# A two-layer hybrid block on one core: the tiles that TensorE reads laid at distances from the weights that are odd multiples of 32 bytes

## What is computed

```python
for l in range(2):
    x = x + 0.5 * swiglu_ffn(rms_norm(x, ffn1_norm[l]), ffn1_w_gu[l], ffn1_w_down[l])     # 1024 -> 2 x 2816 -> 1024
    h = rms_norm(x, mix_norm[l])
    (x_r, g_r, q_b, c_kv, q_i, k_i, w_i, q_c, k_c, v_c, f_c, gate_a, gate_b, gate_c) = split(h @ w_in[l])
    merged = (sigmoid(gate_a) * (rglru_branch(...) @ w_branch[l, 0])
              + sigmoid(gate_b) * (dsa_branch(...) @ w_branch[l, 1])
              + sigmoid(gate_c) * (fox_branch(...) @ w_branch[l, 2]))
    x = x + merged @ w_out[l]
    x = x + memory_cross_attention(rms_norm(x, xattn_norm[l]), rms_norm(mem, mem_norm[l]), w_mq[l], w_mkv[l], w_mo[l])
    x = x + 0.5 * swiglu_ffn(rms_norm(x, ffn2_norm[l]), ffn2_w_gu[l], ffn2_w_down[l])
return rms_norm(x, final_norm)
```

## Time and profile before

| | before |
|---|---|
| median of 3 runs | 1412.49 us (1412.26 to 1412.88) |
| profiled execution | 1413.24 us, span 1411.4 us |
| TensorE: matmuls, weight loads | 97%, 87% of the span |
| VectorE, ScalarE, GpSimd | 67%, 55%, 9% |
| mean granted clock of TensorE | 0.994 |
| memory read | 241 MB, 172 GB/s over the span |

### The profile page before, as it was taken

How to read it: one execution, slowest core, us unless ns; L and a number is a source line. 1 busy time by engine, 2 the same in 40 slices (tenths; PEclk the granted TensorE clock), 3 DMA queues, 4 the chain that set the end, 5 groups by cost and what they waited for, 6 DMA issues and landing times.

```text
span 1411.4 us, 23830 instructions
## 1 busy us (share of the span) xinstructions
PE 1372.3 (97%) x8846; PEld 1224.1 (87%) x8846; DVE 944.3 (67%) x1456; ACT 777.2 (55%) x1378; POOL 131.2 (9%) x219
## 2 busy tenths in 40 slices
PE   6999989999999999999999999999999999999998
PEld 5888879988999888888888888898989989888886
DVE  5666665868666567666676666658777666666665
ACT  5555555745654466454565555466546445655554
POOL 4010000022420100000010000000224001100000
PEclk9999999999999999999999999999999999999999
DMA  8677664544545545666666667446454554466662
GB/s 240 189 205 208 199 177 150 180 125 151 174 135 174 180 139 175 183 193 193 179 179 193 194 178 221 136 138 203 129 162 138 163 195 145 127 207 179 196 190 75
DMA packets 286384, 243.38 MB, mean 172 GB/s; under 512 B 14344, under 2 KB 263608, under 8 KB 286304
## 3 DMA queue, kind: packets, MB, share of 16 engines
q1 hardware_dynamic: 284176, 236.77, 55.5%
q10 hardware_dynamic: 1600, 4.25, 0.9%
q0 software_dynamic: 528, 1.26, 0.5%
HBM read 241.18 MB, written 1.27 MB: 172 GB/s over the span
## 4 chain that ended last, share of the span: by engine, by line
issue 64%; PE 26%; DVE 3%; ACT 2%; POOL 2%; POOLq 1%; DVEq 1%; DMA 1%; ACTq 0%
PE work L1548 16%; PE work L1623 2%; PE work L1570 2%; PE acc L1585 1%; PE work L1627 1%; PE acc L1775 1%; POOL diag L721 1%; ACT w_hi L507 1%; PE work L1763 1%; DVE w_lo L515 1%; POOLq L720 1%; DVE score L1350 1%; PE work L1754 1%; PE work L1698 0%; PE acc L1499 0%
## 5 line engine op out<-in xcount | busy, mean ns | idle before, releaser
L515 DVE TENSOR_TENSOR w_lo<-raw,w_hi 128x1024 fp32r<-128x1024 f32 x444 | 549.6, 1258 | 104.2 <-ACT w_hi L507 102.3
L507 ACT ACTIVATE w_hi<-raw 128x1024 fp32r<-128x1024 f32 (+1 forms) x442 | 450.5, 1053 | 25.6 <-PE acc L1585 25.6
L1623 PE MATMUL work<-act,w_hi 128*128 128x512 f32 x1408 | 439.2, 393 | 9.5 <-DVE w_lo L515 5.5
L1627 PEld LDWEIGHTS work<-act,w_lo 128*128 128x128 f32 x1408 | 265.0, 188 | 59.2
L1548 PE MATMUL work<-act,w_hi 128*128 128x256 f32 x1696 | 312.0, 282 | 4.2 <-DVE act L1131 2.1
L1627 PE MATMUL work<-act,w_lo 128*128 128x256 f32 x1408 | 278.8, 279 | 0.0
L1548 PEld LDWEIGHTS work<-act,w_hi 128*128 128x128 f32 x1696 | 262.2, 188 | 11.0 <-issue 6.2
L1548 PE MATMUL work<-act,w_lo 128*128 128x256 f32 x848 | 236.7, 279 | 0.0
L1623 PEld LDWEIGHTS work<-act,w_hi 128*128 128x128 f32 x1408 | 216.5, 188 | 13.4 <-issue 10.4
L821 ACT ACTIVATE gu_s<-work 128x256 f32<-128x256 f32 x176 | 58.1, 382 | 199.1 <-PE work L1627 199.1
L1548 PEld LDWEIGHTS work<-act,w_lo 128*128 128x128 f32 x848 | 159.1, 188 | 0.6 <-issue 0.5
(11 more groups left out here) (238 smaller groups left out, 1746.0 us busy)
## 6 DMA issues: line engine op xcount, KB each, us to landing
raw<-in_ffn_w_gu SPq DMA_DIRECT2D x174, 512.0 KB, 5.0
raw<-in_w_in SPq DMA_DIRECT2D x52, 1024.0 KB, 5.2
raw<-in_ffn_w_down SPq DMA_DIRECT2D x44, 1024.0 KB, 4.9
raw<-in_w_branch SPq DMA_DIRECT2D x12, 1024.0 KB, 5.0
raw<-in_w_mkv SPq DMA_DIRECT2D x8, 1024.0 KB, 5.2
raw<-in_w_out SPq DMA_DIRECT2D x8, 1024.0 KB, 4.9
raw<-in_w_mq SPq DMA_DIRECT2D x4, 1024.0 KB, 5.4
raw<-in_w_mo SPq DMA_DIRECT2D x4, 1024.0 KB, 4.8
```

What stands on the lines that cost most here:

```text
L507: eng.activation(halves(w_hi, slot, kind, part), halves(raw, slot, kind, part), ACT.Copy)\
L515: eng.tensor_tensor(halves(w_lo, slot, kind, part), halves(raw, slot, kind, part), halves(w_hi, slot, kind, part).bitcast(F32), ALU.subtra ...
L1623: pe.matmul(work[:, 2 * c + g, :], w_hi[:, slot, at_w:at_w + P], act[:, :, k, :], start=(k == 0), stop=False, skip_group_check=True)
L1627: mm = pe.matmul(work[:, 2 * c + g, 0:SEQ], w_lo[:, slot, at_w:at_w + P], act_hi[:, k, :], start=False, stop=(k == KT - 1), skip_group_che ...
```

## The change

The order of the `at` calls. No instruction, wait, size or overlay differs, apart from the addresses. The 320, 224, 64 and 128 bytes of small tiles now lie between the big ones and shift them by 32 bytes modulo 64, and the 8192 bytes of `mem_x` (with `fox_bias` and `mrg_lo` over it) move from before the branch tiles to behind `pt`, the place of the products.

```diff
         x = at("x", [P, TT, D])
-        mem_x = at("mem_x", [P, TT, D])
-        fox_bias = at("fox_bias", [P, HEADS, SEQ], over="mem_x")
-        mrg_lo = at("mrg_lo", [P, KT, SEQ], F32R, over="mem_x")
+        mx = at("mx", [P, 4, 2])
+        nm = at("nm", [P, 4, 2])
+        gain = at("gain", [P, 5, KT])
         xr = at("xr", [P, BT, SEQ + CONV_W])
...
+        gains = at("gains", [P, 5, DEPTH, KT])
         act = at("act", [P, 2, KT, SEQ], F32R)
         act_hi, act_lo = act[:, 0, :, :], act[:, 1, :, :]
+        sm = at("sm", [P, 4, 2])
+        ri = at("ri", [P, 4, 2])
         o_hi0, o_lo0, o_hi1, o_lo1 = (at(name, [P, BT, SEQ], F32R) for name in ("o_hi0", "o_lo0", "o_hi1", "o_lo1"))
...
         lg = at("lg", [P, 2, 2, SEQ])
+        ch = at("ch", [P, 8, BT])
         pt = at("pt", [P, 2, 2, 2, P])
+        mem_x = at("mem_x", [P, TT, D])
+        fox_bias = at("fox_bias", [P, HEADS, SEQ], over="mem_x")
+        mrg_lo = at("mrg_lo", [P, KT, SEQ], F32R, over="mem_x")
...
-        gains = at("gains", [P, 5, DEPTH, KT])
-        gain = at("gain", [P, 5, KT])
-        ch = at("ch", [P, 8, BT])
...
-        mx = at("mx", [P, 4, 2])
-        nm = at("nm", [P, 4, 2])
-        sm = at("sm", [P, 4, 2])
-        ri = at("ri", [P, 4, 2])
```

## The result

The changed kernel takes 1429.18 us (median; 1427.44 to 1430.02) against 1412.38 before: a ratio of 1.0122, 95% interval 1.011 to 1.0135. It is slower by 17 us, where 24 us less had been forecast; the range held the time. The profiled execution has a span of 1428.2 us, 16.8 more than before.

The account below looks back on a forecast made before the run. The prediction took the pace of successive TensorE matmuls as the bound, not memory or waits. Gate and up 7.2, down 2.3, last down and output projections 2.5 and L1548 12.0 us summed to 24.0: 1412.5 - 24.0 = 1388.5 us, range 1372 to 1434.

Parts of the forecast that it names:

- (c): Tiles of VectorE, ScalarE and GpSimd move by 32 modulo 64: at most 3 us either way, taken as 0.
- (d): mem_x, fox_bias and mrg_lo go behind the products, small tiles fill gaps; same overlays and waits: 0.
- (a): Four big matmul groups move to distance 160 modulo 256; lower-end paces of 113.3 and 226.6 ns save 24.0 us.
- (b): Branch tiles moving, memory parts and act as stationary operand get other distances; counted nothing, bounds 5.7 us gain, 1.2 us cost.
- odd multiples of 32 are the bad phase: Rival, same four groups: one stall more per step, 21.7 us slower, 1434 us; chance 0.22.
- The distance doesn't count: Rival: starting phase or tile sizes set the matmuls' pace, so time stays 1412.5 us within 3; chance 0.15.
- the third rival: Stalls vanish altogether: fast-form matmuls reach the plain fp32 pace, 216.7 and 108.3 ns, 82 us less, 1330 us; chance 0.08.
- My picture of two reads that stall each other: Reading the next matmul's weights meets the running moving-operand read; short stalls explain pace differences of 3 to 7 ns.

Follow-up runs that it names:

- the sweep: TensorE matmuls alone on zeros, 24 per distance from 0 to 992 bytes: 512 columns take 229 ns at 192, 233 to 234 at most others.
- the two halves of the change: Kernel before with act alone moved: 1424.56 us, ratio 1.009; changed kernel with act back at 192: 1416.0 us, ratio 1.0024 to the kernel before.
- the last sweep: TensorE alone, moving operand alternating between two starts, then 248 to 512 columns, then plain float32: 256 columns at 192 took 113.3 ns over 24 steps.
- two sweeps: TensorE alone over distances, in steps of 32, then in steps of 8: gate and up pattern at 224 took 693.5 and 706.8 ns.

## Why the prediction was wrong

**What bounds the kernel: right.** The pace of the matmuls is the time. The waits of TensorE stayed where they were, and all engines' tiles could move by 32 modulo 64 for nothing, (c) and (d) of the prediction.

**That the pace goes with the distance modulo 256: right for this kernel's steps**, and shown by the sweep, by the two halves of the change and by the kernel with everything 32 bytes up. One shape at one clock takes 226.5 or 233.5 ns by addresses alone, and kernel and sweep agree on the size for 512 columns. It isn't the whole: at 256 columns what ran before and the moving operand's step change the pace as much. The plain form takes 215.8 ns at every distance.

The Trainium skill's rule ("SBUF — State Buffer", who interferes with whom), by which TensorE waits on nobody, is about other engines, and there the sweep agrees: 5.60 and 5.50 us at 160 and 192 with VectorE and ScalarE busy, 5.61 and 5.50 with both idle. That addresses don't matter, as the prediction drew from it, doesn't follow; the difference is there with TensorE alone. The Trainium skill's 2.5 ns over the columns' time for one matmul behind another ("TensorE: Matmul & The Clock Gate", back-to-back issue gap) agree with the plain form if a record counts as twice its columns, 213.3 and 426.7 ns, and not with the fast form.

**The step that failed is (a), the choice of the end.** The cost at 160 had been bounded by 113.3 and 120.0 ns (226.6 and 233.2), and I took the lower end because 160 is next to 192 and because 0 and 64 seemed the bad places. That took a curve for smooth of which three points were known, and read one of them wrongly: 0 is bad for 256 columns (120.0), but for 512 it is the best multiple of 32 (226.5). The merged sums, which mix 0 and 64, had hidden it. The sweep has it: from 192 to 160, 512 columns go from 229 to 233.5 and 256 columns from 117.8 to 120. The measured paces are at the upper bound in each of these groups. What the 113.3 of the earlier trace rows shows is a rhythm that a sequence at 192 can fall into, over 24 steps in the last sweep; at 160 the same unit takes 120.0.

Term by term, in the profile after:
- gate and up: 88 x 0.12 = 10.6 us more (forecast 7.2 less).
- down: 960 x 4.0 ns = 3.8 us more (forecast 2.3 less).
- last down and the output projections: the same within 0.02 us in 22 steps (forecast 2.5 less). They came from 64 and went to 160, both at 233.
- L1548 with act: 2544 x 2.0 ns = 5.1 us more (forecast 12.0 less).
- (b), counted at nothing: the branch tiles gain 576 x 0.4 ns, 0.2 us.

This makes 19.3 us, where the profiled span grew by 16.8. Added up from start to start over the whole of both traces, gate and up take 9.7 us more, the down projection 3.4 and L1548 with act 5.8, the branch tiles 0.2 less. Against these stands L1570 with act, 28.2 us after and 31.1 before. The mean granted clock in 18 us around one such unit is 0.91 after and 0.81 before, which goes with it.

**The rivals.** The second, "odd multiples of 32 are the bad phase", had the outcome and nearly the price: blocks of 5.65 us, 21.7 us in all, against 5.64 and 17. Its reason was wrong. Reads that begin 32 bytes past a multiple of 64 cost nothing by themselves (all tiles 32 bytes up: 0.9999), and 224, odd as well, is 2 us from the best. It had 0.22 and the forecast 0.46, when bounds that lie equally far from the present value, for a quantity that isn't known to be smooth, give no reason to prefer one. "The distance doesn't count" is out as an account of the change, though the phase in which a sequence starts, which it named, does count beside the distance (113.3 and 117.8 ns at 192). The pace of the plain form (the third rival's) was not reached at any of the distances tried with 512 columns.

**My picture of two reads that stall each other** carried the distance but not more. With a quarter of the weights to load the cost per matmul stays at 18 to 20 ns, and it changes with the moving operand's own step and with what ran before. No row names a stall. What the 7 to 20 ns are, and why 0 and 192 are the good places for 512 columns, stays open.

## What to carry to other kernels

Where matmuls in the fast float32 form follow one another with no waits, measure the distance between start and start for each pair of operands, and compare it over the kernel: places with one shape and two paces may point to the placement. A pace measured at some distances says nothing of a distance between them; a sweep of 24 matmuls per distance costs one run and gives the curve. It is safest for one long shape: for the gate and up pattern and for 256 columns two sweeps gave two paces at some distances, so the kernel itself has to be run. Here the best placement tried was 192 for the weights over act and 0 for the products over the weights, 2.5 us below the kernel before, and no rule of odd or even would have found it.

## What the runs showed that I had not expected

- The pace repeats every 256 bytes of distance, and good and bad places lie 32 bytes apart: 512 columns take 229 ns at 192 and 233.5 at 160.
- The sign matters. At 256 columns 160 gives 120.0 ns and 96, its mirror image, 117.3 to 118.6.
- Several rhythms exist at one distance: at 224 four matmuls of the gate and up pattern took 693.6 ns in one sweep and 707 in the other, 694 in the kernel; at 160 it was 700 in the sweep, once it ran evenly, and 706.5 in the kernel.
- Matmuls of 248 columns and more in the fast float32 form have 7 to 20 ns over the columns' time, mostly 10 or more; a record in the plain form has 2.5 over the time of twice its columns.
